# Reading the moving operand of the large products from the last column to the first, and writing PSUM in the same order

## The chip, the cores and the metric

The kernel runs on one core of one Trainium2 chip. What is compared is the device time of one execution in microseconds (us), the median of the runs of a kernel.

## What is computed

A chain of transformer layers on one sequence of 256 tokens with 2048 features, all in float32. The weight products make up nearly all of the work:

```python
def pool_layer(x, mem, ...):                 # layer 0
    h = rmsnorm(x, norm_g); proj = h @ w_in  # 2048 -> 4096
    y_pool = multiscale_pool(u, w_pool, pool_scale) * silu(zu)
    y_mem = memory_attention(qm, mem, mem_g, w_mem_kv) * silu(zm)
    return x + concatenate([y_pool, y_mem]) @ w_out
...
def nsa_layer(x, mem, ...):                  # layer 1: attention over compressed, selected
    ...                                      # and windowed keys, and memory attention
    return x + concatenate([y_nsa, y_mem], axis=-1) @ w_out
...
def second_block(x, ...):                    # three kinds of attention, then the FFN
    qkv = einsum('bsd,de->bse', h, w_qkv[l])
    x = x + einsum('bse,ed->bsd', y, w_o[l])
    g = causal_dwconv(einsum('bsd,df->bsf', h, w_gate[l]), conv_w[l], conv_b[l])
    u = einsum('bsd,df->bsf', h, w_up[l])
    x = x + einsum('bsf,fd->bsd', silu(g) * u, w_down[l])
```

## The kernel before

The program is written out by hand for each engine, with semaphores between them. TensorE's program is one long list in a fixed order. Nothing is scheduled by a planner: the function `plan` only counts the weight units and says which PSUM bank each tile takes.

**Numbers in two parts.** Each float32 number of a large product is kept as a high part and a low part, both in the type fp32r, and the product of two numbers is made from three partial products: high by high, high by low, low by high. An activation tile for one of the KT = 16 slices of features is 128 partitions by T = 256 tokens, and its high and low parts lie in `RH`, `RY` or `HID` as [128, 2, k, 256]. `both(R)` gives three views of slice k: the high part alone, both parts (a pattern of two blocks of 256 columns), and the low part alone.

**Weights.** They stream from HBM through 699 units (ACT's queue brings the first one, SP's the others) of mostly 128 x 1024 numbers into the staging buffer `s_stage`. ScalarE writes the high part of a unit into `s_w` (line 1156), VectorE the low part (line 1726). There are three slots for such units, each `WH` and `WL`. TensorE waits for a unit (`wl`) and counts it as used (`units`).

**Tile products** (`tile` and `b_unit`, lines 544 to 569). The weights are the stationary operand (128 x 128), the activations are the moving operand. For each slice, line 554 multiplies the high weights with both activation parts, 512 columns, into the whole PSUM bank of 512 columns; line 555 multiplies the low weights with the high activations, 256 columns, and adds them to the upper half of the same bank. A unit of 1024 weight columns is eight such pairs of instructions. The reader of the bank (VectorE) adds the two halves afterwards.

**Group products** (`group`, lines 571 to 602). The same two matmuls (lines 595 and 598), but four output tiles at once in four banks, so that the first products of a layer can begin with the first slices of a norm.

**Value products** (`pair`, lines 604 to 629). Here tokens are the rows of the output, so activations (128 x 128) are stationary and the weights are moving: three matmuls of 512 columns for each slice and token half, lines 621, 622 and 623, all into the same bank and the same 512 columns. `SHIFT` moves these weights by 8 columns in their slot.

**What else runs on TensorE.** Pool products (`three`, lines 537 to 539), the compression (line 752), the gate (line 798), attention scores, transposes, values and norms. Most of the attention products are plain float32, where the profile shows two records for each matmul of the program.

The weight loads (LDWEIGHTS) are not written in the program: each matmul brings one, and it appears in the profile under the same line, as the engine PEld.

Of the kernel before, what the change touches and what calls it, by code (L numbers as in the profile page):

```python
# [16 lines left out]
T = 256  # L17
# [495 lines left out]
    return banks[2 * q + t]  # L513


def both(R):
    return lambda k: (R[:, 0, k, :], R[:, :, k, :], R[:, 1, k, :])


def tensor_program(e, S, P, M):  # L520
# [4 lines left out]
    def vacant(*banks):  # L525

        for b in banks:
            if b in held:
                w.wait_ge(*held[b])

    def unit():
        done[0] += 1
        side.tick()
# [7 lines left out]
    def ready(name, base=0):  # L541
        return lambda k: w.wait_ge(name + "l", base + k + 1)

    def b_unit(o, nk, k0, first, last, x, ready, mw=128):
        c = done[0]
        r = c % NR
        if c:
            w.wait_ge("wl", c + 1)
        for kk in range(nk):
            ws = slice(kk * mw, kk * mw + mw)  # L550
            ready(k0 + kk)
            xh, xx, _ = x(k0 + kk)
            begin, end = first and kk == 0, last and kk == nk - 1
            e.matmul(o, M.WH[:, r, ws], xx, start=begin, stop=False)  # L554
            m = e.matmul(o[:, T:2 * T], M.WL[:, r, ws], xh, start=False, stop=end)  # L555
        m.then_inc(S["units"], 1)

    def tile(t, x, ready, sizes=(8, 8), k0=0, mw=128):

        bank = P.bank[t]  # L560
        vacant(bank)
        held[bank] = P.out[t]
        k = k0
        for n, nk in enumerate(sizes):
            b_unit(M.product(bank)[0:mw, :], nk, k, n == 0, n == len(sizes) - 1, x, ready, mw)
            k += nk
            if n == len(sizes) - 1:
                assert done[0] + 1 == P.end[t], t
            unit()

    def group(tiles, x, ready, hook=None):

        for u in range(8):
            c = done[0]
            r = c % NR
            if c:
                w.wait_ge("wl", c + 1)
            if u >= 6:
                steps = [(12 + n % 4, 2 * u - 12 + n // 4, n) for n in range(8)]
            elif u or not c:  # L580
                steps = [(2 * u + n // 4, n % 4, n) for n in range(8)]
            else:
                steps = [(kk, p, 4 * kk + p) for p in (2, 3, 0, 1) for kk in range(2)]
            for k, p, n in steps:
                ws = slice(128 * n, 128 * n + 128)
                if k == 0:
                    vacant(P.bank[tiles[p]])
                    held[P.bank[tiles[p]]] = P.out[tiles[p]]
                if u in (0, 6, 7) or p == 0:
                    ready(k)  # L590
                o = M.product(P.bank[tiles[p]])
                xh, xx, _ = x(k)
                if c == 0:
                    w.wait_ge("wh" if n >= 4 else "wh_a", 1)
                e.matmul(o[:, :], M.WH[:, r, ws], xx, start=k == 0, stop=False)  # L595
                if c == 0:
                    w.wait_ge("wl" if n >= 4 else "wl_a", 1)
                m = e.matmul(o[:, T:2 * T], M.WL[:, r, ws], xh, start=False, stop=k == 15)  # L598
            m.then_inc(S["units"], 1)
            if hook is not None and u == 3:  # L600
                hook()
            unit()

    def pair(t, x, ready):

        banks = [P.bank[t, i] for i in range(2)]
        vacant(banks[0])
        for u in range(8):
            c = done[0]
            r = c % NR  # L610
            w.wait_ge("wl", c + 1)
            steps = [(kk, i) for i in range(2) for kk in range(2)] if u in (0, 7) else [(kk, i) for kk in range(2) for i in range(2)]
            for n, (kk, i) in enumerate(steps):
                if u == 0 and n == 2:
                    vacant(banks[1])
                k = 2 * u + kk
                ready(k)
                xh, _, xl = x(k)
                ts, ws = slice(128 * i, 128 * i + 128), slice(SHIFT + 512 * kk, SHIFT + 512 * kk + 512)
                o = M.product(banks[i])  # L620
                e.matmul(o[:, :], xh[:, ts], M.WH[:, r, ws], start=(k == 0), stop=False)  # L621
                e.matmul(o[:, :], xh[:, ts], M.WL[:, r, ws], start=False, stop=False)  # L622
                m = e.matmul(o[:, :], xl[:, ts], M.WH[:, r, ws], start=False, stop=(k == 15))  # L623
                if u == 7 and n == 1:
                    m.then_inc(S["half"], 1)
            m.then_inc(S["units"], 1)
            unit()
        for i in range(2):
            held[banks[i]] = P.out[t, i]
# [330 lines left out]
    def diff_head(h):  # L960
# [32 lines left out]
        head_norm(n, ones, 128)  # L993

    H, Y = both(M.RH), both(M.RY)
    H0 = H


    side.start(token_rows("mem_c", 15))
    group([("mk", 0, j) for j in range(4)], H, ready("m0"))  # L1000
    pair(("mv", 0), H, ready("m0"))
    side.start(lam())
    side.start(token_rows("x_c", 13))
    group([("mk", 1, j) for j in range(4)], Y, ready("m1"))
    pair(("mv", 1), Y, ready("m1"))


# [28 lines left out]
    def kv_hook():  # L1036
        w.wait_ge("sqk", KT)
        norm_rows("kv", [(ones, M.ACC[0][:, :])])
        side.start(kv_cols())

    group([("kc", j) for j in range(4)], H, ready("kv"), kv_hook)
    side.start(compress())
    for j in range(4):
        tile(("vc", j), H, ready("kv"))
    for n in ("ks", "kw"):
        for j in range(4):
            tile((n, j), H, ready("kv"))
    pair("vs", H, ready("kv"))
    pair("vw", H, ready("kv"))
    side.drain()  # L1050
# [52 lines left out]
    for hv in range(2):  # L1103
        first = 22 * hv
        if hv == 0:
            group([(n, j) for j in range(2) for n in ("wg", "wu")], Y, ready("hf"), ffn_hook)
            first = 2
        for j in range(first, 22 * hv + 22):
            tile(("wg", j), Y, ready("hf"))
            tile(("wu", j), Y, ready("hf"))  # L1110
        residual(("wd", hv), both(M.HID), ready("hid", 22 * hv), (0, 1, 2), 2, (8, 7, 7))
# [1786 lines left out]
```

## Time and profile before

| what | value |
|---|---|
| median of 3 runs | 2039.43 us (2038.6 to 2040.6) |
| span of the profiled execution, first to last instruction | 2037.8 us |
| TensorE matmul busy | 2019.6 us, 11506 instructions |
| TensorE weight load busy | 1763.8 us, 11506 instructions |
| VectorE, ScalarE, GpSimd busy | 1452.9, 1036.3, 415.8 us |
| mean granted TensorE clock | 0.996 of full |
| HBM traffic | 372 MB, 183 GB/s over the span |

The profiled execution has no own time besides its span; its span is 1.6 us below the median of the runs and 0.8 us below the shortest of them. Matmuls are pipelined: the duration of one in the profile (390 ns for 512 columns) contains the time that it overlaps with its neighbours. What a matmul costs in a stream is the time from its start to the start of the next one, and the prediction works with such differences of start times.

### The profile page before, as it was taken

What the parts mean: (1) busy time and instruction counts of PE and PEld (TensorE: products, weight loads), DVE (VectorE), ACT (ScalarE), POOL (GpSimd) and SP (SyncE); (2) the same over time, 40 slices, a digit from 0 to 9 for tenths busy, and PEclk for the clock granted to TensorE, in tenths of its full rate; (3) what the DMA queues carried; (4) which work ended last, traced back from release to release, by engine and by line L of the source; (5) the groups of instructions that cost most, each with busy time, mean ns of one, the idle gap of its engine ahead of it and who ended that gap; (6) DMA issues with size and microseconds to landing.
All of it is one profiled execution on the core that took longest, in us unless ns stands there. A gap on an engine that the chain in (4) does not pass through costs nothing.

```text
span 2037.8 us, 29295 instructions
## 1 busy us (share of the span) xinstructions
PE 2019.6 (99%) x11506; PEld 1763.8 (87%) x11506; DVE 1452.9 (71%) x2056; ACT 1036.3 (51%) x1548; POOL 415.8 (20%) x376
## 2 busy tenths in 40 slices
PE   8999999999999999999999999999999999999998
PEld 7888888888888888888878888888888888888887
DVE  6866788788796556876656678777776567777755
ACT  6744544566433554644555555455454344545443
POOL 0014553300000344430122235211010000101122
PEclk9999999999999999999999999999999999999999
DMA  9664556567654334555444445555556655555664
GB/s 339 218 193 151 193 186 196 184 226 239 210 182 145 114 114 135 187 203 189 152 161 141 154 149 190 183 191 190 190 190 187 190 191 190 192 191 192 183 189 145
DMA packets 104809, 374.22 MB, mean 184 GB/s; under 512 B 11840, under 2 KB 13152, under 8 KB 104288
## 3 DMA queue, kind: packets, MB, share of 16 engines
q1 hardware_dynamic: 104384, 371.83, 54.8%
q8 instruction: 91, 1.49, 0.3%
q10 hardware_dynamic: 288, 0.52, 0.1%
q14 instruction: 46, 0.38, 0.0%
HBM read 370.21 MB, written 2.10 MB: 183 GB/s over the span
## 4 chain that ended last, share of the span: by engine, by line
PE 94%; DVE 3%; DMA 1%; ACT 1%; POOL 0%; issue 0%; DVEq 0%; SPq 0%; ACTq 0%
PE psg L554 50%; PE psg L555 26%; PE psg L621 2%; PE psg L623 2%; PE psg L622 2%; PE psg L595 1%; PE pst L595 1%; DVE s_w L1726 1%; PE pst L752 1%; PE psg L598 1%; PE pst L598 1%; PE pss L843 1%; PE pst L660 1%; DMA s_stage<-in_mk 1%; PE pso L863 1%; ACT s_w L1156 0%
## 5 line engine op out<-in xcount | busy, mean ns | idle before, releaser
L1726 DVE TENSOR_TENSOR s_w<-s_stage,s_w 128x1024 fp32r<-128x1024 f32 (+3 forms) x698 | 861.4, 1236 | 350.8 <-ACT s_w L1156 348.0
L1156 ACT ACTIVATE s_w<-s_stage 128x1024 fp32r<-128x1024 f32 (+3 forms) x698 | 727.0, 1043 | 730.6 <-PE psg L555 633.6
L554 PE MATMUL psg<-s_ry,s_w 128*128 128x512 f32 x2560 | 900.4, 394 | 1.8 <-DVE s_qc L1780 1.8
L555 PE MATMUL psg<-s_ry,s_w 128*128 128x256 f32 x2560 | 723.2, 283 | 0.0
L554 PEld LDWEIGHTS psg<-s_ry,s_w 128*128 128x128 f32 x2560 | 482.5, 188 | 108.0 <-issue 2.3
L555 PEld LDWEIGHTS psg<-s_ry,s_w 128*128 128x128 f32 x2560 | 485.8, 190 | 0.4
L554 PE MATMUL psg<-s_rh,s_w 128*128 128x512 f32 x1216 | 428.0, 394 | 0.3 <-DVE s_w L1726 0.3
L555 PE MATMUL psg<-s_rh,s_w 128*128 128x256 f32 x1216 | 342.7, 282 | 0.0
L554 PEld LDWEIGHTS psg<-s_rh,s_w 128*128 128x128 f32 x1216 | 228.3, 188 | 49.0 <-issue 1.0
L554 PE MATMUL psg<-s_hid,s_w 128*128 128x512 f32 x704 | 244.1, 390 | 0.0
L555 PEld LDWEIGHTS psg<-s_rh,s_w 128*128 128x128 f32 x1216 | 229.8, 189 | 0.7
L555 PE MATMUL psg<-s_hid,s_w 128*128 128x256 f32 x704 | 198.5, 282 | 0.0
L2599 POOL TENSOR_TENSOR s_hid<-s_hh,s_hid 128x256 fp32r<-128x256 f32 x44 | 52.8, 1200 | 563.1 <-ACT s_hid L1528 563.1
L554 PEld LDWEIGHTS psg<-s_hid,s_w 128*128 128x128 f32 x704 | 132.2, 188 | 27.7
L555 PEld LDWEIGHTS psg<-s_hid,s_w 128*128 128x128 f32 x704 | 133.1, 189 | 0.0
L2484 POOL TENSOR_SCALAR s_bsc<-s_bsc,s_stat 128x256 f32<-128x256 f32 (+1 forms) x56 | 45.2, 826 | 193.0 <-DVE s_stat L2142 181.8
L1969 DVE TENSOR_TENSOR s_x<-psg,s_x 128x256 f32<-128x256 f32 x112 | 47.2, 421 | 34.0 <-PE psg L555 33.4
L2477 POOL TENSOR_TENSOR s_psq<-s_x 128x256 f32<-128x256 f32 x44 | 41.1, 935 | 131.9 <-DVE s_x L1971 131.9
L621 PE MATMUL psg<-s_w,s_ry 128*128 128x512 f32 x160 | 64.8, 405 | 1.4 <-DVE s_w L1726 1.2
L2489 POOL TENSOR_TENSOR s_rh<-s_yt,s_rh 128x256 fp32r<-128x256 f32 x32 | 40.6, 1270 | 116.3 <-ACT s_rh L1196 116.3
L623 PE MATMUL psg<-s_w,s_ry 128*128 128x512 f32 x160 | 62.5, 391 | 0.0
L622 PE MATMUL psg<-s_w,s_ry 128*128 128x512 f32 x160 | 62.5, 390 | 0.0
(417 smaller groups left out, 2203.4 us busy)
## 6 DMA issues: line engine op xcount, KB each, us to landing
s_stage<-in_wo SPq DMA_DIRECT2D x96, 512.0 KB, 3.6
s_stage<-in_wg SPq DMA_DIRECT2D x84, 512.0 KB, 3.5
s_stage<-in_wu SPq DMA_DIRECT2D x84, 512.0 KB, 3.9
s_stage<-in_ain SPq DMA_DIRECT2D x64, 512.0 KB, 3.7
s_stage<-in_wd SPq DMA_DIRECT2D x64, 448.0 KB, 3.3
s_stage<-in_wkv SPq DMA_DIRECT2D x32, 512.0 KB, 3.6
s_stage<-in_wd SPq DMA_DIRECT2D x32, 512.0 KB, 3.4
s_stage<-in_bq SPq DMA_DIRECT2D x24, 512.0 KB, 3.6
```

What stands on the lines that cost most here:

```text
L554: e.matmul(o, M.WH[:, r, ws], xx, start=begin, stop=False)
L555: m = e.matmul(o[:, T:2 * T], M.WL[:, r, ws], xh, start=False, stop=end)
L595: e.matmul(o[:, :], M.WH[:, r, ws], xx, start=k == 0, stop=False)
L621: e.matmul(o[:, :], xh[:, ts], M.WH[:, r, ws], start=(k == 0), stop=False)
L622: e.matmul(o[:, :], xh[:, ts], M.WL[:, r, ws], start=False, stop=False)
L623: m = e.matmul(o[:, :], xl[:, ts], M.WH[:, r, ws], start=False, stop=(k == 15))
L1156: e.activation(M.weights(c, 0, n, shift), M.staged(c, n), ACT.Copy).then_inc(S["wh"], 1)
L1726: e.tensor_tensor(M.weights(c, 1, n, shift), M.staged(c, n), M.weights(c, 0, n, shift), ALU.subtract).then_inc(S["wl"], 1)
L1969: chain(e.tensor_tensor(M.X[:, j, :], b[:, T:2 * T], M.X[:, j, :], ALU.add))
L2477: chain(e.tensor_tensor(b, src, src, ALU.mult))
L2484: x = e.tensor_scalar(ap, ap, scale, None, ALU.mult)
L2599: e.tensor_tensor(M.HID[:, 1, i, :], M.HH[j % 2][:, :], M.HID[:, 0, i, :].bitcast(F32), ALU.subtract).then_inc(S["hidl"], 1)
```

## The change

All matmuls of the tile, group and value products get patterns that run backwards: the moving operand is read from its last column to its first, and PSUM is written from the last column to the first. Each column still meets the same weights and lands in the same place. A moving operand of two blocks is reversed in both dimensions, so the low activation part is read first, backwards, then the high part. The stationary operands, the number of instructions, their order, the semaphores, the buffers and all other engines' programs stay.

```diff
+def back(a):
+
+    return a[:, ::-1] if len(a.shape) == 2 else a[:, ::-1, ::-1]
...
-            e.matmul(o, M.WH[:, r, ws], xx, start=begin, stop=False)
-            m = e.matmul(o[:, T:2 * T], M.WL[:, r, ws], xh, start=False, stop=end)
+            e.matmul(back(o), M.WH[:, r, ws], back(xx), start=begin, stop=False)
+            m = e.matmul(back(o[:, T:2 * T]), M.WL[:, r, ws], back(xh), start=False, stop=end)
...
-                e.matmul(o[:, :], M.WH[:, r, ws], xx, start=k == 0, stop=False)
+                e.matmul(back(o[:, :]), M.WH[:, r, ws], back(xx), start=k == 0, stop=False)
...
-                m = e.matmul(o[:, T:2 * T], M.WL[:, r, ws], xh, start=False, stop=k == 15)
+                m = e.matmul(back(o[:, T:2 * T]), M.WL[:, r, ws], back(xh), start=False, stop=k == 15)
...
-                e.matmul(o[:, :], xh[:, ts], M.WH[:, r, ws], start=(k == 0), stop=False)
-                e.matmul(o[:, :], xh[:, ts], M.WL[:, r, ws], start=False, stop=False)
-                m = e.matmul(o[:, :], xl[:, ts], M.WH[:, r, ws], start=False, stop=(k == 15))
+                e.matmul(back(o[:, :]), xh[:, ts], back(M.WH[:, r, ws]), start=(k == 0), stop=False)
+                e.matmul(back(o[:, :]), xh[:, ts], back(M.WL[:, r, ws]), start=False, stop=False)
+                m = e.matmul(back(o[:, :]), xl[:, ts], back(M.WH[:, r, ws]), start=False, stop=(k == 15))
```

## Rows read from the trace of the kernel before

**Rows 1.** Page, part 4: the chain that ended last, by engine and line.
```profile
PE 94%; DVE 3%; DMA 1%; ACT 1%; POOL 0%; issue 0%; DVEq 0%; SPq 0%; ACTq 0%
```
**Rows 2.** Windows: stretch, each engine's busy time, TensorE clock, DMA share, GB/s.
```profile
0.00:100.00 100.00, 92.34 (x456) 78.20 (x457) 74.91 (x133) 74.15 (x130) 0.64 (x9) 1.00 0.78 282
...
660.00:1540.00 880.00, 877.27 (x5030) 758.95 (x5030) 612.21 (x875) 455.86 (x755) 233.17 (x217) 1.00 0.49 167
1540.00:2025.00 485.00, 485.00 (x2800) 429.97 (x2800) 325.63 (x417) 222.88 (x265) 57.16 (x52) 1.00 0.58 186
```
**Rows 3.** Groups by form, TensorE: line, shapes, xcount, busy us, mean ns, idle before.
```profile
L554 PE MATMUL psg<-s_ry,s_w 128*128 128x512 f32 x2560 | 900.4, 394 | 1.8 <-DVE s_qc L1780 1.8
...
L554 PE MATMUL psg<-s_rh,s_w 128*128 128x512 f32 x1216 | 428.0, 394 | 0.3 <-DVE s_w L1726 0.3
...
L554 PE MATMUL psg<-s_hid,s_w 128*128 128x512 f32 x704 | 244.1, 390 | 0.0
...
L621 PE MATMUL psg<-s_w,s_ry 128*128 128x512 f32 x160 | 64.8, 405 | 1.4 <-DVE s_w L1726 1.2 <-DVE s_vb L1793 0.2
...
L621 PE MATMUL psg<-s_w,s_rh 128*128 128x512 f32 x96 | 37.8, 394 | 0.8 <-DVE s_w L1726 0.8
...
L595 PE MATMUL psg<-s_ry,s_w 128*128 128x512 f32 x96 | 35.6, 399 | 0.0
L595 PE MATMUL pst<-s_ry,s_w 128*128 128x512 f32 x96 | 34.9, 391 | 0.0
...
L595 PE MATMUL psg<-s_rh,s_w 128*128 128x512 f32 x64 | 25.0, 416 | 6.5 <-DVE s_rh L1744 6.5
L595 PE MATMUL pst<-s_rh,s_w 128*128 128x512 f32 x64 | 24.3, 405 | 0.0
```
**Rows 4.** Timeline, TensorE, full clock: start us, duration us, what.
```profile
1499.72 0.39 PE L554 MATMUL psg<-s_ry,s_w 128*128 128x512 f32 x1
1499.95 0.28 PE L555 MATMUL psg<-s_ry,s_w 128*128 128x256 f32 x1
1500.07 0.39 PE L554 MATMUL psg<-s_ry,s_w 128*128 128x512 f32 x1
...
1507.69 0.39 PE L554 MATMUL psg<-s_ry,s_w 128*128 128x512 f32 x1
```
**Rows 5.** Timeline, TensorE, at 630 us, then the granted clock there.
```profile
629.66 0.63 PE L554 MATMUL psg<-s_ry,s_w 128*128 128x512 f32 x1
630.08 0.41 PE L555 MATMUL psg<-s_ry,s_w 128*128 128x256 f32 x1
...
631.58 0.63 PE L554 MATMUL psg<-s_ry,s_w 128*128 128x512 f32 x1
...
629.00:634.40 5.40, 5.40 (x20) 4.58 (x20) 4.14 (x16) 0.69 (x3) 0.00 (x0) 0.54 0.03 12
```
**Rows 6.** Timeline, TensorE, two value products: first and last rows used.
```profile
1075.82 0.39 PE L621 MATMUL psg<-s_w,s_ry 128*128 128x512 f32 x1
...
1078.31 0.39 PE L623 MATMUL psg<-s_w,s_ry 128*128 128x512 f32 x1
...
1083.24 0.40 PE L623 MATMUL psg<-s_w,s_ry 128*128 128x512 f32 x1
...
1085.31 0.39 PE L623 MATMUL psg<-s_w,s_ry 128*128 128x512 f32 x1
```
**Rows 7.** The chain in order of time: plain float32 matmuls (256, 128 columns), compression.
```profile
763.84 0.87 PE pss L695 x4
...
666.12 0.66 PE pst L660 x6
...
429.87 0.92 PE pst L752 x4
```
**Rows 8.** Timeline, TensorE weight loads beside the matmuls of rows 4.
```profile
1499.95 0.19 PEld L554 LDWEIGHTS psg<-s_ry,s_w 128*128 128x128 f32 x1
1500.07 0.19 PEld L555 LDWEIGHTS psg<-s_ry,s_w 128*128 128x128 f32 x1
1500.30 0.19 PEld L554 LDWEIGHTS psg<-s_ry,s_w 128*128 128x128 f32 x1
```

## Prediction

> **What bounds the kernel now.** I read the chain that ended last first: 94% of it is TensorE [rows 1]. The table by stretch says how tightly: from 1540 to 2025 us TensorE shows no idle time at all (485.00 of 485.00), from 660 to 1540 it idles 2.7 us of 880; only the first 100 us have waits worth the name, 7.7 us [rows 2]. The other engines have room: VectorE, the busiest of them, works 325.63 of 485 us in the last stretch, and DMA 58% [rows 2]. So whatever a matmul gains or loses between its start and the next start goes into the time almost undiluted, and nothing else does.
>
> Next, how much of TensorE the change touches. By form, line 554 ran 2560 + 1216 + 704 = 4480 times and line 595 ran 96 + 96 + 64 + 64 = 320 times; lines 555 and 598 follow each of these once, so there are 4800 pairs of 512 and 256 columns. Line 621 ran 160 + 96 = 256 times, and lines 622 and 623 as often: 768 value matmuls [rows 3]. That is 10,368 of the 11,506 matmuls.
>
> The durations there (394 ns) overlap, so I take starts. From 1499.72 to 1507.69 us lie 23 pairs: 346.5 ns a pair [rows 4]. The value products show 11 steps between 1075.82 and 1078.31, 226 ns for 512 columns [rows 6]. 4800 x 0.3465 + 768 x 0.226 = 1837 us, 90% of the span. All forecasts below are this span plus what the change adds; the span (2037.8) is 1.6 us below the median of the runs, and I add those 1.6.
>
> **What a pair's 346.5 ns are made of.** At 630 us the granted clock is at its lower level for most of a stretch (mean 0.54 of full, so mostly 1.2 GHz, after the attention of this stage kept TensorE on small products). There three pairs take 1.92 us, 640 ns each [rows 5]. 768 columns in 640 ns are 1.2 columns per ns: one per clock, nothing on top. At full clock the same columns would be 320 ns, but the pair takes 346.5. So at full clock there are 13 ns on top of each matmul, 256 or 512 columns long, which do not show at half clock: something beside the array, which does not run faster with its clock, is at its limit. Plain float32 matmuls are no such case: a record of 256 columns takes 0.87 / 4 = 217 ns and one of 128 takes 0.66 / 6 = 110 ns [rows 7], the columns twice over plus 3 ns. They ask for a new moving column half as often. The 13 ns thus belong to the fast reading (or writing) of four-byte columns. They are not quite fixed either: nine steps of the value product from 1083.24 to 1085.31 take 230 ns each against 226 elsewhere [rows 6], and the four compression matmuls 0.92 / 4 = 230 [rows 7], with the same number of columns. The weight load of the next matmul runs at the same time from the same memory (0.19 us, begun as the current matmul starts) [rows 8].
>
> **The change, part by part.**
> - Removed: nothing. Added: nothing; instructions, waits and buffers are the same, so no semaphore, queue or DMA moves. Cost 0 by construction, not by a cover.
> - The operand of line 554 jumps once between its two blocks, backwards now. The jump costs little forwards: in rows 4 the step after line 554 (1499.72 to 1499.95) is 0.23 us, as that of a value matmul without a jump. I take 0 for it.
> - Line 555 adds into columns that line 554 wrote just before. Forwards, column 256 is written 256 columns after its first writing; backwards, column 511 comes 512 columns after. The distance only grows there, and at the next pair's start it falls from 512 to 256, what it was in the other place. I take 0.
> - The rate of a backward stream, in reading and in writing. No row of this trace shows a backward pattern, so it is bounded. Above: each changed column at one per 0.83 ns, the half-clock rows. Pairs 640 - 346.5 = 293.5 ns, times 4800, 1409 us; value matmuls 0.42 us (line 554's step at 630.08) less 0.226, times 768, 149 us; together +1558 us. Below: the 13 ns fall to the 3 ns of plain float32. A pair would be 217 + 110 = 327 ns, 19 less, 91 us over 4800; 9 ns less for 768 value matmuls, 7 us; together -98 us. Between these far ends I take 0: two neighbouring columns are neighbours in memory in either order, blocks begin and end on even columns, and the jump shows that the stream is not bound to one long ascending run. The sum is 0.
>
> The Trainium skill speaks against that: "PSUM — Partial Sum Buffer", Specifications, gives PSUM cachelines of 8 bytes and says that any non-contiguous access pattern slows matmuls significantly. No run here shows whether contiguous but descending counts as such. If it does, the sum is nearer the upper bound of +1558 us than 0; if the line alone counts, which is how "Advanced Engine Details and Errata", PSUM Cachelines, has it for each two consecutive elements, it is 0.
>
> **The rivals.** One measure for all: 0.2% of the time is 4.1 us, about what a measurement of this kernel can tell from no change, and over 10,368 matmuls that is 0.4 ns each. Anything at all that the direction does to the 13 ns will be seen.
>
> *Much slower (0.16).* The unit that fetches columns, or the one that adds them into PSUM, joins two neighbours only when the second address is the higher one. Then both neighbours cost a slot each and the stream falls to the half-clock rate. Place: every changed matmul. It decides as soon as one of read and write is built so. Time 2037.8 + 1558 + 1.6 = 3597 us. For it: the pair is at the limit of something already, so there is no slack to hide it. Against: the jump inside line 554 costs nothing visible.
>
> *A little slower (0.21).* The 13 ns come from moving reads and weight loads that meet in the memory, and the meeting depends on how the two streams run: now both ascend, afterwards they run against each other. The rows show a step between two states of 230 - 226.4 = 3.6 ns [rows 6]. If every changed matmul goes to the worse one, +37 us: 2077 us. For it: the step itself, and that the compression sits at 230 with its own addresses.
>
> *A little faster (0.28).* The same mechanism the other way: streams that ascend together can hold each other up again and again, and streams that run against each other pass once. The same step of 3.6 ns gives -37 us, 2002 us; the most is the lower bound, 1941 us. For it: 10 of the 13 ns are absent wherever the moving stream is slower, so there is something to win. Against both small rivals: over the 23 pairs the cadence is constant although addresses, slots and the work of VectorE and ScalarE change, which also fits a fixed start-up of each stream that has no direction. The Trainium skill, "TensorE: Matmul & The Clock Gate", Step-by-step, gives TensorE two independent read ports and says that loading weights takes no read bandwidth from the running matmul; by that both would be 0. The trace agrees in the cadence, not in the 226 and 230.
>
> *No change (0.35).* The 13 ns are such a start-up, and a backward stream is as good as a forward one. Time 2037.8 + 0 + 1.6 = 2039.4 us.
>
> **How the numbers follow.** No change is the likeliest single case, so the forecast is 2039.4 us, and its own range is 2035 to 2044. The range must leave out the much slower case (0.16) and little else: on the fast side it goes past the step (2002) but not to the full bound (1941), since losing all 10 ns needs every meeting gone: 1980. On the slow side past 2077 to 2090. Faster 0.28, same 0.35, slower 0.21 + 0.16 = 0.37. Cases of both signs together hold more than the likeliest one, and the middle of the range is the case with no effect.
>
> **What would show it.** In the timeline at full clock: 346.5 ns a pair means no effect, 339 or 354 the small ones, 327 the lower bound, 640 and more the upper. If the cause is on the reading side, the weight loads' durations (0.19 us) should move too. If reading and writing both matter with opposite signs, the sum hides it, and only kernels that reverse one of them can tell. At half clock, around 630 us, the small rivals predict the old 640 ns, since there the array is the bound. If pairs shorten and the total does not, then VectorE has become late with its half of the weights; at 67% busy [rows 2] I do not expect it. The prediction is wrong if the cadence moves by more than 0.4 ns, and badly wrong if a backward stream is a slow one.

## The result, and the profile after

The changed kernel takes 2059.22 us (median of 4 runs, 2058.28 to 2060.56) where the kernel before, beside it, takes 2039.01 (2037.12 to 2040.6): ratio 1.0104, 95% interval 1.0091 to 1.0116. I had forecast no change, and it is 1% slower. The medians are 20.2 us apart. The profiled execution spans 2056.5 us, before 2037.8: 18.7 us more, and it is these 18.7 that the traces have to explain.

The page's part 1 (busy time and instructions of each engine) and the TensorE end of part 4 (the chain) of the changed kernel:

```profile
PE 2040.4 (99%) x11506; PEld 1755.5 (85%) x11506; DVE 1454.8 (71%) x2056; ACT 1034.8 (50%) x1548; POOL 412.8 (20%) x376
```
```profile
PE 94%; DVE 3%; DMA 2%; ACT 1%; issue 0%; SPq 0%; DVEq 0%; ACTq 0%
```

TensorE has the 94% of [rows 1], DMA 2% instead of 1%, and the number of instructions is the same: no engine has taken TensorE's place. The table of stretches, with the same columns as [rows 2]:

```profile
0.00:100.00 100.00, 93.31 (x456) 77.30 (x457) 74.97 (x134) 74.02 (x130) 0.64 (x9) 1.00 0.79 282
660.00:1540.00 880.00, 878.18 (x4988) 749.25 (x4988) 607.24 (x869) 452.36 (x755) 230.14 (x217) 1.00 0.51 165
1540.00:2025.00 485.00, 485.00 (x2765) 422.85 (x2764) 325.94 (x420) 220.23 (x264) 53.81 (x49) 1.00 0.61 187
```

TensorE still shows no idle time in the last stretch, but gets through 2765 matmuls there instead of 2800 in the same 485 us. From 660 to 1540 us it idles 1.8 us instead of 2.7. So the loss lies inside the matmuls. Their starts show it. The timeline at full clock, first two pairs and the start of the 24th (start, duration, what):

```profile
1499.70 0.40 PE L559 MATMUL psg<-s_ry,s_w 128*128 128x512 f32 x1
1499.94 0.28 PE L560 MATMUL psg<-s_ry,s_w 128*128 128x256 f32 x1
1500.06 0.40 PE L559 MATMUL psg<-s_ry,s_w 128*128 128x512 f32 x1
...
1507.78 0.40 PE L559 MATMUL psg<-s_ry,s_w 128*128 128x512 f32 x1
```

23 pairs in 8.08 us: 351.3 ns, where [rows 4] gives 346.5. The value products, first and last of 22 steps in the same view:

```profile
84.83 0.40 PE L626 MATMUL psg<-s_w,s_ry 128*128 128x512 f32 x1
...
89.96 0.40 PE L627 MATMUL psg<-s_w,s_ry 128*128 128x512 f32 x1
```

5.13 us / 22 = 233.2 ns a step against 226 in [rows 6]. And at half clock, where the table gives a clock of 0.50 for 634.40 to 637.60:

```profile
634.45 0.63 PE L559 MATMUL psg<-s_ry,s_w 128*128 128x512 f32 x1
...
637.01 0.63 PE L559 MATMUL psg<-s_ry,s_w 128*128 128x512 f32 x1
```

Four pairs in 2.56 us, 640 ns each, as in [rows 5]: at half clock the change costs nothing. The extra time shows only at full clock, like the 13 ns a matmul that the prediction found on top of the column count.

**Does that account for the loss?** Means over the whole trace (every step from the start of one of these matmuls to the start of the next, without waits and without the stretches at the lower clock, over 9,000 of them; computed from the starts in the trace) are 346.75 ns a pair before and 351.2 after; for the value products, their first steps after an interruption included, 228.5 and 233.4. That is 4800 x 4.45 = 21.4 us and 768 x 4.9 = 3.8 us, together 25.2, and 18.7 are seen. Two terms come back. Up to its last matmul this execution spent 3.4 us at the lower clock, that of before 10.2 (6.8 at 630 us, 3.4 at 907): 6.8 us less, of which half, 3.4 us, is won. And waits swallowed about 2: TensorE's idle time fell from 7.7 to 6.7 us in the first 100 us, from 1.0 to 0.8 from 100 to 600, from 2.7 to 1.8 from 660 to 1540. 25.2 - 3.4 - 2.1 = 19.7, a microsecond from the 18.7.

### The profile page after: what moved, and what is told of

It is laid out like the page before. It is cut to its first block, busy times and chain, and to the rows that moved or that the text cites. A ratio compares the mean times of both kernels' runs of the same rounds, so it can differ in the third digit from the quotient of the medians.

```text
span 2056.5 us, 29295 instructions
## 1 busy us (share of the span) xinstructions
PE 2040.4 (99%) x11506; PEld 1755.5 (85%) x11506; DVE 1454.8 (71%) x2056; ACT 1034.8 (50%) x1548; POOL 412.8 (20%) x376
## 4 chain that ended last, share of the span: by engine, by line
PE 94%; DVE 3%; DMA 2%; ACT 1%; issue 0%; SPq 0%; DVEq 0%; ACTq 0%
PE psg L559 51%; PE psg L560 26%; PE psg L626 3%; PE psg L627 2%; PE psg L628 2%; DVE s_w L1731 1%; PE psg L600 1%; DMA s_stage<-in_mk 1%; PE pst L600 1%; PE pst L757 1%; PE pss L848 1%; PE pst L665 1%; PE pso L868 1%; PE pst L603 0%; PE psg L603 0%; DMA s_stage<-in_mv 0%
## 5 line engine op out<-in xcount | busy, mean ns | idle before, releaser
L559 PE MATMUL psg<-s_rh,s_w 128*128 128x512 f32 x1216 | 433.1, 401 | 0.1
```

The lines of the kernel that those rows point to most:

```text
L559: e.matmul(back(o), M.WH[:, r, ws], back(xx), start=begin, stop=False)
```

## The experiments

All ran beside the kernel before. Each result is the ratio of its time to that of the kernel before, with the 95% interval. "Pair" and "value" are the trace's means as just defined; a value step counts as settled when the steps around it repeat. As a second, coarser witness each kernel's row for 1560 to 2020 us stands below where the verdict rests on it: 460 us without idle time, so its count of matmuls is the cadence (460 us over half the count). The kernel before has x2656 there (346.4 ns a pair), the changed one x2622 (350.9).

### Read or write, columns or blocks: e1 to e4

```diff
 e1_read_only, as on each changed line:
-e.matmul(back(o), M.WH[:, r, ws], back(xx), ...)
+e.matmul(o, M.WH[:, r, ws], back(xx), ...)
 e2_write_only:
+e.matmul(back(o), M.WH[:, r, ws], xx, ...)
 e3_within, in back(): blocks of 256 keep their order, columns in them turned
+return a[:, :, ::-1]         (512 contiguous columns: as two blocks of 256)
 e4_blocks, in back(): blocks swapped, columns in them ascending
+return a[:, ::-1, :]         (256 columns: unchanged)
```

In e1 and e2 only one side of each product is turned, so columns land in mirrored places; the amount of work is the same.

> The moving operand of the tile, group and value products is read backwards, PSUM is written forwards, so the columns of these products land in mirrored places and the output is not the reference's. Theory R (the price is paid where the moving operand is read): as the changed kernel, 2059 us, ratio to before 1.010; 512 columns 233 ns start to start instead of 228, 256 columns 118 as before. Theory W (it is paid where PSUM is written): 2039 us, ratio 1.000, pair 346.5 ns. Theory B (only read and write in opposite or equal direction matters): this kernel and the one that only writes backwards differ from both.

> The moving operand is read forwards, PSUM is written backwards in the same products; columns land in mirrored places, the output is not the reference's. Theory R: 2039 us, ratio 1.000, pair 346.5 ns. Theory W: 2059 us, ratio 1.010, pair 351 ns. If both sides pay a part, the ratios of this kernel and of the one that only reads backwards add up to 1.010 (for instance 1.005 each).

> The output stays the reference's. Each block of 256 columns is read and written backwards, but the two blocks of the 512 column matmuls of lines 554 and 595 keep their order (high part first); the value products read their 512 weight columns in one piece backwards as in the change and write two blocks of 256, each backwards, in the forward order of the blocks, so that here the mapping of columns differs from the reference. If descending addresses are the cause: 2059 us, 512 columns 233 ns. If the backward jump between the blocks or the order of the parts is the cause: 2039 us for the tile and group products, only the value products (at most 768 x 6.5 ns = 5 us) still slower, ratio up to 1.0025.

> Within each block of 256 columns everything ascends as before; only the order of the two blocks of the 512 column matmuls of lines 554 and 595 is swapped (low part first), and PSUM is written in that order. The value products read forwards as before but write the upper block of 256 first, which mirrors blocks against the reference. If descending addresses are the cause: 2039 us, pair 346.5 ns. If the backward jump or the order of the parts is: 2059 us, 512 columns 233 ns.

One remark in the expectations of e3 and e4 is mistaken: in the value products too, both sides were turned in the same blocks, so nothing is computed otherwise. The windows of e1 and of e2:

```profile
1560.00:2020.00 460.00, 460.00 (x2622) 400.61 (x2621) 307.95 (x395) 208.55 (x250) 50.41 (x46) 1.00 0.61 188
```
```profile
1560.00:2020.00 460.00, 460.00 (x2656) 407.81 (x2655) 309.67 (x393) 212.39 (x253) 55.08 (x51) 1.00 0.62 187
```

Measured: e1 1.0111 (1.0095 to 1.0128), pair 351.2, value 233.4. e2 1.0002 (0.9992 to 1.0011), pair 346.7, value 228.6. e3 1.0113 (1.0098 to 1.0128), pair 351.2. e4 1.0000 (0.9991 to 1.001), pair 346.7. It is the reading, and in it the descending run of columns. Writing PSUM from last to first is free here, and so is jumping between blocks.

### Which of the two matmuls: e8

```diff
 e8_256_only: only the second matmul of a pair is turned
+e.matmul(o, M.WH[:, r, ws], xx, ...)
 m = e.matmul(back(o[:, T:2 * T]), M.WL[:, r, ws], back(xh), ...)
```

> Only lines 555 and 598 (256 columns, low weights by high activations) run backwards; all 512 column matmuls forwards as before. The output stays the reference's. The changed kernel showed 118 ns for them in either direction. If a backward read costs only in its own matmul and only from 512 columns on: ratio 1.000, pair 346.5 ns. If it disturbs the stream behind it (the compression and pool products, which were not changed, became 2 ns and 1 ns slower there too), the forward 512 column matmuls rise as well: up to 233 ns, ratio up to 1.010.

Measured: 0.9996 (0.9987 to 1.0006). The timeline:

```profile
1499.63 0.39 PE L559 MATMUL psg<-s_ry,s_w 128*128 128x512 f32 x1
...
1503.79 0.39 PE L559 MATMUL psg<-s_ry,s_w 128*128 128x512 f32 x1
```

12 pairs in 4.16 us, 346.7 ns. In the mean the unturned 512 columns now take 231.7 ns (228 before) and the turned 256 take 115.4 (118): a matmul's step also depends on its neighbour, and the two shifts cancel. In the changed kernel the 512 columns take 233 and the 256 still 118.

### Is the price in the direction, or in the places? e5, e6, e7

In the kernel before, a row of split weights starts 128 bytes past a multiple of 256, the activations 160 past: counted modulo 256, the moving operand of a tile product stands 32 bytes from the weights that TensorE loads meanwhile. The length of a filler buffer sets this "tile distance" (moving minus stationary start, modulo 256). SHIFT, the first column of the weights that the value products use, sets their distance, which is 0 in the kernel before.

```diff
 e5_fwd_start64 (before.py) and e6_back_start64 (the changed kernel):
-SHIFT = 8
+SHIFT = 0
-self.PAD = fix("pad", [128, (128 + 32 - ...) % 256 // 4])
+self.PAD = fix("pad", [128, (128 + 64 - ...) % 256 // 4])
 e7_all_32_on (changed kernel): ahead of every buffer, and 64 as above
+self.PAD0 = fix("pad0", [128, 8])
```

e5 and e6 have tile distance 64 and value distance -64; e7 moves everything by 32 bytes, distances as they were.

> The kernel before, reading forwards, with the activations (and all buffers behind them) 32 bytes further up and SHIFT = 0, so that each moving operand of the tile, group and value products starts at a multiple of 64 bytes; before, it started 32 bytes past one. The output stays the reference's. Theory P (what a stream costs depends on where in 64 bytes it starts, forwards or backwards): slower than before, 512 columns at about 230 ns, which the compression (which starts at a multiple of 64) shows in the kernel before: +3 ns x 5568 = 17 us, ratio 1.008. Theory D (the descending direction itself costs, wherever it starts): no change, ratio 1.000.

> The changed kernel (all reads and writes backwards) with the same 32 bytes: the moving operands lie between multiples of 64 bytes. The output stays the reference's. Theory P: differs from the changed kernel's 1.010, either way; if the backward stream has its good place here, 512 columns at 227 to 228 ns and ratio 1.000. Theory D: as the changed kernel, ratio 1.010, 512 columns 233 ns.

> The changed kernel with 32 bytes in front of all buffers, so that weights and activations move together: starts are multiples of 64 bytes for the moving operands, but the distance between moving and stationary operands is that of the changed kernel. The output stays the reference's. If the absolute place of the moving operand counts: as e6_back_start64. If the place of the moving operand relative to the weights that are loaded meanwhile counts: as the changed kernel, 1.010, whatever e6_back_start64 shows. Theory D: 1.010 in both.

The windows of e5, then of e7:

```profile
1560.00:2020.00 460.00, 460.00 (x2638) 402.87 (x2638) 308.67 (x394) 210.60 (x250) 50.49 (x46) 1.00 0.59 189
```
```profile
1560.00:2020.00 460.00, 460.00 (x2622) 400.62 (x2621) 307.28 (x393) 208.89 (x249) 50.68 (x46) 1.00 0.59 188
```

Measured: e5 1.0100 (1.0083 to 1.0117), pair 350.9, value 233.3; e6 1.0148 (1.0133 to 1.0163), pair 353.3; e7 1.0106 (1.0091 to 1.0121), pair 351.2. e5 is the turning point of the study: the forward kernel, with no column turned, loses the same 1% when its operands stand elsewhere (64 instead of 32 in the tile products, -64 instead of 0 in the value products). e7 says that moving both operands together by 32 bytes changes nothing: the absolute place doesn't count.

### The map of distances: e9 to e16

Same two lines edited (PAD `128 + X`, and SHIFT), with the changed kernel or that of before:

```diff
 e9_back_t0:    X = 0,   SHIFT = 8      e10_back_t224: X = 224, SHIFT = 8
 e11_back_t128: X = 128, SHIFT = 24     e12_fwd_t0:    X = 0,   SHIFT = 8
 e13_back_t96:  X = 96,  SHIFT = 28     e14_back_t192: X = 192, SHIFT = 44
 e15_back_t160: X = 160, SHIFT = 8      e16_fwd_t96:   X = 96,  SHIFT = 24
```

> The changed kernel with the activation buffers 32 bytes lower: moving operands of the tile products start at the same place within 256 bytes as the weights (distance 0; the changed kernel has 32, e6_back_start64 has 64); value products: weights move, at 32 bytes from their activations (the changed kernel has 0). The output stays the reference's. Theory S (the price comes from moving reads and weight loads that meet in the memory, and depends on their distance and on the direction): a ratio other than 1.010; if the backward stream has a distance as good as the forward stream's 32, it must be found at one of 0, 128 and 224, with 512 columns at 228 ns and ratio 1.000. Theory D (a backward stream costs 5 to 10 ns more wherever it lies): 1.010 or more here and in the two beside it.

> As e9_back_t0, but the activations lie 224 bytes past the weights' place (that is 32 before the next), the mirror image of the changed kernel's 32; value products at distance 64. The output stays the reference's. If turning the stream around mirrors the pattern of distances: ratio 1.000, 512 columns 228 ns. If not: 1.010 or more (theory D), or something else (theory S without a mirror).

> As e9_back_t0 with distance 128, and SHIFT = 24, value products at distance -32. The output stays the reference's. If the pattern repeats every 64 or 128 bytes, this equals e9_back_t0 in the tile products; if every 256, it need not.

> The kernel before, all reads forwards, at the distance 0 of e9_back_t0. The output stays the reference's. Theory S: slower than before, as distance 64 was (1.010); anywhere from 1.000 to 1.015. Theory D for the direction alone: e9_back_t0 is slower than this one by the same 1.010 as the changed kernel is than before, since the place is the same in both.

> The changed kernel with the activations 96 bytes past the place of the weights within 256 bytes, SHIFT = 28: value products at distance 16. The output stays the reference's. Theory S-lost (the kernel before sat at a distance made for a forward stream; a backward stream has none as good, or not at 32 bytes and at 0): backward pairs measured so far are 351.2 (distance 32, 224) and 353.3 ns (0, 64, 128); here one of these, or 346.7 and ratio 1.000 if this is the backward stream's good place. Value products: 233.4 ns as at the five other distances, or 226.7 if 16 is their good place.

> As e13_back_t96 with distance 192, value products at -16. Theory S-lost: pair 351 to 353 ns, value 233.4 ns, ratio 1.010 to 1.016. A good place for the backward stream would show as 346.7 and 226.7 ns.

> As e13_back_t96 with distance 160 (the changed kernel's 32 plus 128), value products at 128 (0 plus 128). If the pattern repeats every 128 bytes: pair 351.2 ns as the changed kernel, ratio 1.010. With e11_back_t128 against e9_back_t0 (both 353.4 ns) this would be the second pair of distances that agree.

> The kernel before, forwards, tile distance 96, but SHIFT = 24 so that the value products keep their distance 0 at another place. Theory S: value products stay at 226.7 ns in long runs (they were 233.2 at 32 and 233.3 at -64), since only the distance counts; tile pairs somewhere between 346.7 and 353 ns. If absolute places counted for them, they would rise to 233. A pair below 346.7 ns would make a kernel faster than before.

All results by tile distance (backward: moving operand read from last to first):

| distance, bytes | backward: pair ns, ratio (interval) | forward: pair ns, ratio (interval) |
|---|---|---|
| 0 | 353.4, 1.0156 (1.0141 to 1.0172) e9 | 348.6, 1.0048 (1.0031 to 1.0064) e12 |
| 16 | not run | 352.0, 1.0112 (1.0095 to 1.0129) e18 |
| 32 | 351.2, 1.0104 (1.0091 to 1.0116) the change | 346.75, before |
| 64 | 353.3, 1.0148 (1.0133 to 1.0163) e6 | 350.9, 1.0100 (1.0083 to 1.0117) e5 |
| 96 | 353.3, 1.0148 (1.0131 to 1.0165) e13 | 350.1, 1.0070 (1.0055 to 1.0085) e16 |
| 128 | 353.4, 1.0146 (1.0131 to 1.0161) e11 | not run |
| 160 | 351.1, 1.0102 (1.0087 to 1.0117) e15 | not run |
| 192 | 351.1, 1.0108 (1.0093 to 1.0123) e14 | not run |
| 224 | 351.1, 1.0102 (1.0086 to 1.0117) e10 | not run |

And by the distance of the value products, ns per 512 columns: backward 233.4 at 0, 32, -32, 64 and -64, 233.6 at 16 (e13), 235.5 at -16 (e14), 234.2 at -128 (e15); forward 226.7 once settled at 0, 233.2 at 32 (e12), 233.3 at -64 (e5). The timelines of e5 and of e16, twelve steps each:

```profile
83.15 0.39 PE L622 MATMUL psg<-s_w,s_ry 128*128 128x512 f32 x1
...
85.95 0.39 PE L622 MATMUL psg<-s_w,s_ry 128*128 128x512 f32 x1
```
```profile
83.05 0.39 PE L622 MATMUL psg<-s_w,s_ry 128*128 128x512 f32 x1
...
85.78 0.39 PE L622 MATMUL psg<-s_w,s_ry 128*128 128x512 f32 x1
```

2.80 us / 12 = 233 ns at distance -64, 2.73 / 12 = 227.5 at distance 0, the latter with both operands 64 bytes from where the kernel before has them, and both in the forward direction.

Three things follow. Backward tile pairs know two levels, 351.1 and 353.4, and no distance on the grid of 32 bytes gives them the 346.7 that forward has at 32. (The pattern doesn't repeat every 128 bytes: 64 has 353.3 and 192 has 351.1.) Forward varies more, and at equal distance backward is dearer by 4.8, 4.4, 2.4 and 3.2 ns a pair (0, 32, 64, 96). But in the value products backward costs 233.4 where forward costs 233.2 or 233.3, except at distance 0, where forward has 226.7. So the direction isn't a fixed price per column; there it loses a good place and nothing else.

### Whose traffic is it? e17, and a finer step, e18

```diff
 e17_fwd_others (before.py): fillers ahead of the staging buffer, the split
 weights and the residual; weights and activations end where they were
+self.PAD0 = fix("pad0", [128, 8])
+self.PAD1 = fix("pad1", [128, 56])
+self.PAD2 = fix("pad2", [128, 8])
 e18_fwd_t16 (before.py): weights 16 bytes up, value distance still 0
-SHIFT = 8
+SHIFT = 4
-slots = fix("w", [128, NR, 2 * UWP], F32R)
+room = fix("w", [128, NR * 2 * UWP + 8], F32R)
+slots = room[:, 4:4 + NR * 2 * UWP].rearrange("p (r c) -> p r c", r=NR)
```

> The kernel before, forwards. Staging buffers, residual, constants, vectors, norm and temporary buffers are moved 32 bytes against the split weights and against the activation buffers; weights and activations keep their distance of 32 (both 256 bytes further up). The output stays the reference's. If only the place of the moving operand against the weights that TensorE loads counts: pair 346.7 ns, ratio 1.000. If it was the place against the buffers that VectorE, ScalarE or DMA use, which every shifted kernel so far changed too: slower, pair 348 to 351 ns, ratio 1.005 to 1.010.

> The kernel before, forwards, with the split weights 16 bytes further up, so tile distance 16; SHIFT = 4 keeps the value products' distance 0. The output stays the reference's. Value products 226.7 ns as before. Tile pairs: distances 0 and 32 gave 348.6 and 346.7 ns; if 16 is a better place than 32, below 346.7 (each ns is 4.8 us, ratio 0.9976), else between or above. Chance of a faster kernel put at one in four.

The windows of e17, then of e18 (its last row looks at an earlier stretch):

```profile
1560.00:2020.00 460.00, 460.00 (x2656) 407.81 (x2656) 309.30 (x393) 212.16 (x254) 53.94 (x49) 1.00 0.61 188
```
```profile
1560.00:2020.00 460.00, 460.00 (x2605) 402.05 (x2604) 305.75 (x392) 208.07 (x248) 48.79 (x44) 1.00 0.61 187
825.00:890.00 65.00, 65.00 (x377) 57.24 (x376) 53.53 (x70) 42.68 (x70) 27.07 (x30) 1.00 0.59 188
```

Measured: e17 0.9995 (0.9986 to 1.0005), pair 346.7, the count of before to the last matmul. e18 1.0112 (1.0095 to 1.0129), pair 352.0, value 228.5. In e17 the staging buffer, the residual, the constants and the temporary buffers have new places against both operands, and nothing moves. One kind of traffic keeps its place there: what ScalarE and VectorE write into the split weights themselves. The trace of e5 settles that one. From 1345 to 2025 us, the 102 pairs beside which nobody writes `s_w` take 348.9 ns, and the 1170 pairs beside which it is written throughout take 348.9 as well; in the kernel before both kinds take 346.7. What is left is where TensorE's own two streams stand to each other, the moving columns and the weights that it loads for the next matmul. Sixteen bytes are enough to turn the best forward distance into the dearest forward one (352.0 in the mean), with the value products, whose distance was kept, at 228.5 as before.

### One distance, several cadences

The means of the forward kernels in the table hide something that the traces show. The windows of e12 (distance 0):

```profile
310.00:400.00 90.00, 90.00 (x511) 78.09 (x510) 70.90 (x84) 40.57 (x48) 36.98 (x36) 1.00 0.58 188
1560.00:2020.00 460.00, 460.00 (x2655) 402.29 (x2654) 309.52 (x394) 212.31 (x252) 51.91 (x47) 1.00 0.61 190
```

From 1560 us on, e12 is as fast as the kernel before (x2656). From 310 to 400 us it makes x511 where the kernel before makes x520. Both stretches are tile products from the same buffers at the same distance. From start to start a pair takes 353.3 ns in the first and 346.7 in the last. e18 does the reverse: 353.3 ns in both these stretches, but 346.7 from 825 to 890 us, where its x377 is also the count of the kernel before. e5 has 353.3 and 348.9. The kernel before (346.7), e16 (350.0) and the backward kernels (351.1 or 353.3) keep one value in all long stretches. At distances 0 and 64 the dearer forward value is just the backward one. So the distance sets which cadences a stretch can have and not always which one it gets. What picks it at the start of a stretch, no run here separates.

## Why the prediction was wrong

- **The step that failed** is "The rate of a backward stream, in reading and in writing", with its bounds of -98 and +1558 us: "Between these far ends I take 0". For writing, 0 is right (e2). For reading it measures +4.4 ns a pair and +4.9 ns a value step in the mean, before what the clock and the waits give back. My reason was that neighbours are neighbours in either order; the trace had already spoken against the premise that nothing but the neighbours counts, with 226 and 230 ns for the same instruction [rows 6]. The term measured 25 us where I had 0.
- **The reading of the 13 ns** as "a fixed start-up of each stream that has no direction" fell with e5: the same forward program takes 350.9 ns a pair with its operands 32 bytes further apart. At least a part of this surplus depends on how the two reading streams stand to each other. How much of them would be left without any meeting, no run shows.
- **The rival "a little slower"** (0.21) named the side and, as far as exclusion shows it, the mechanism. Its size was off: +3.6 ns for every changed matmul, +37 us. Measured, a pair grows by 4.4 and not 7.2 ns; the 256-column half keeps its 118. The value steps grow by 4.9 and not 3.6. The 230 in [rows 6] was not a second steady state either, but a mean over a series that was still settling: its nine steps are 236, 224, 231, 236, 228, 232, 231, 227 and 227 ns, and longer series go on with 227, 227, 226. After an interruption up to some ten matmuls pass until then. That the cadence depends on the relative timing of two streams would explain it; it is not shown.
- **"A little faster"** (0.28) rested on the idea that opposed streams meet once and aligned ones again and again. The table says the reverse in the mean at all four distances where both were run.
- **The Trainium skill**, "TensorE: Matmul & The Clock Gate", Step-by-step, with its two independent read ports, would have both small rivals at 0. The measurement speaks against it for these float32 streams: 346.7 against 350.9 ns a pair by moving one of the two streams 32 bytes (e5). The rule of the Trainium skill, "PSUM — Partial Sum Buffer", Specifications, on non-contiguous patterns, which I had set against my 0, doesn't take in contiguous descending writes: e2, 1.0002.
- **Right were**: nothing for the jump between blocks (e4) and for the order of rewriting in PSUM (e2); 640 ns at half clock; VectorE not late (its busy share 71%, TensorE idle less than before). The count 10,368 of changed matmuls and the measure "0.4 ns each is 0.2%" held as well.
- **A sign that misled**: I had written that a cause on the reading side should move the weight loads' durations. They stay at 0.19 us [rows 8] in every run (means between 187.6 and 189.7 ns). Why only the steps of the matmuls grow, no run shows, and it leaves the part of the weight load without a trace of its own.

Unchanged products inherited some of it: the compression's steps went from 231.4 to 233.5 ns, three of the four series of pool products from 116.7 to 117.8, with their own code untouched. Whether that is their weight load meeting a turned neighbour has not been separated.

**Not settled.** How the memory's places are laid out, and why 512 columns pay and 256 don't. That weight load and moving read are the pair that meets is by exclusion: e7 excludes absolute place, e17 and the writes beside e5's pairs the other engines, e2 the writing of PSUM; the direction and speed of the weight load itself were not varied. What picks the cadence of a stretch in e12, e18 and e5 is open; it fits a race of two streams and shows that a mean over one window is one sample. Backward tile products were tried only at multiples of 32 bytes, so a good place for them on a finer step isn't excluded: forwards, 16 bytes changed much.

No version beats the kernel before: e8 (0.9996) and e17 (0.9995) equal it. Of the five forward distances measured, it stands at the best one.

## What to carry to other kernels

When TensorE is at 99% with a constant surplus over its column count that vanishes at half clock, as here, don't take the surplus for a fixed start-up: move the moving operand against the stationary one by 16 or 32 bytes and time it before changing anything else. Look at the cadence of several stretches, not of one. A bound that gives "no effect" needs the same evidence as one that gives an effect; two cadences for one instruction in one trace are evidence that something matters. Turn outputs and not inputs where a reversed order is wanted: writing PSUM from last to first was free here, reading SBUF so was not.

## What the runs showed that I had not expected

- The relative place of the two operands, in steps of 16 bytes, moves the whole kernel by 0.5 to 1.1% with the same instructions in the same order and direction (e12, e16, e5, e18: 1.0048, 1.0070, 1.0100, 1.0112).
- A matmul that is not turned takes 231.7 ns instead of 228 because its neighbour is (e8), and the neighbour gives the same time back.
- The time at the lower clock differs from one profiled execution to the next: 3.4 us in the changed kernel against 10.2 before. It is no effect of the change, for it is 10.2 us in e9, the slowest kernel, and 3.4 in e4, as fast as the kernel before; but it has to be taken out of the sum.
- Long stretches of the same products at the same distance run at 346.7 ns a pair in one place and 353.3 in another (e12, e18).
